# Moving the modulation vector of a transformer kernel from its own TensorE stage into the mixing stage, on VectorE

## The chip, the cores and the metric

One NeuronCore of a Trainium2 chip runs the whole kernel. The metric is the device time of one execution in microseconds (us), the median of three runs. The engines are TensorE (PE, its weight loads PEld), VectorE (DVE), ScalarE (ACT), GpSimd (POOL) and the sync engine (SP), which issues the weight transfers in program order.

## The reference, cut to what matters

256 tokens of width 1024 pass through two blocks. All is float32.

```
h = x
xn = rmsnorm(h); proj = xn @ w_in                  # "mixing": attention and a gated recurrence
h = h + concat(attn, rec) @ w_out                  # outproj
hn = rmsnorm(h)
# PEER: product keys, top 16 of 8 heads -> 128 rows of u and of v for every token
eidx, gates = topk(hn @ wq, subkeys)
act = gelu(sum_d(hn * u[eidx]));  h = h + sum_k(gates * act * v[eidx])
h = rmsnorm(h)
# second block, two layers, each modulated by six vectors that depend on c alone
m = silu(c) @ ada_w + ada_b                        # [1024] @ [1024, 6144], once for each layer
x = modulated mixer, modulated swiglu (layer 0) ; modulated attention, modulated swiglu (layer 1)
```

The change concerns `m`. It needs only `c` and two matrices of 25 MB each, and is first used behind the PEER stage.

## The kernel before

Features lie on the 128 partitions, tokens on the free axis. Weights come in units of 1 MB (2048 columns on 128 partitions) or 1.5 MB (3072 columns) into `ring`, which has four slots. SP loads unit g when unit g-4 has been used (`wait_slot`, semaphore `unit_done`). The list `LAYERS` gives the order: `inproj` is units 0 to 13, `outproj` 14 to 17, `peerq` 18 to 25, `ada` 26 to 57, and then the second block.

**Mixing.** PE works through units u = 0 to 13: `unit_start(u)`, then `features` or `rows` (32 passes of 128x256), then for u from 4 on a `level(u-4)` of the recurrence and pieces of the attention: `at_transpose`, `at_scores`, `at_out`. On DVE a loop over u from 4 to 13 goes beside it: read the bank of unit u, `level_diff(i+1)`, `level_keep(i)` with i = u-4, `at_logits(u-8)`, `at_norm(u-9)`; behind the loop stand `at_norm(5)`, four `at_store` and the recurrence's output. ACT takes exponentials (`level_exp`, `at_exp`), POOL two products for each level (L363, L364). Ahead of the loop, DVE forms the forget gates (from L755) once ACT has read units 2 and 3, and `level(0)` hangs on these.

**Outproj, peerq.** DVE adds each outproj unit to `hT` (L887); `norm(1)` follows, then eight peerq units, transposes, and the scores (L1398).

**Top-k and gather.** DVE finds the top 16 for both halves of the tokens. POOL then fetches rows by indirect DMA (L381), 512 times 128 rows of 4 KB into `rows`, a ring of 12 buffers: phase 0 and 2 from `u_d` (DVE L960), phase 1 and 3 from `v_d` (DVE L968). A buffer is refilled when DVE has used it. The first 12 are fetched while DVE is still busy with the second half's top-k.

**Modulation before.** Behind the scores PE runs 32 `ada` units: eight matmuls of one column of `silc` against 384 columns of weights (L1411), giving one row of 384 in PSUM; ACT copies it (L534), and three matmuls with one partition turn it into three columns (L1420, into `psum[:, MCOL_AT+...]`). DVE adds the bias to the 96 columns after phase 0 (L986) and forms four gains (L989).

```
dve.wait_ge(row_in[n % GRING], 16 * (n // GRING + 1))
v.tensor_tensor_reduce(row, row, xrow[tt], 1.0, 0.0, ALU.mult, ALU.add, S["act"][:, tt, k:k + 1])
```

Of the kernel before, what the change touches and what calls it, by code (L numbers as in the profile page):

```python
# [40 lines left out]
LAYERS = [("inproj", 14), ("outproj", 4), ("peerq", 8), ("ada", 32), ("l0in", 10), ("l0out", 4),  # L41
# [6 lines left out]
UNIT_COLS = {"ada": 3072, "ffn0": 3072, "ffn1": 3072}  # L48
RING = 4
RING_COLS = 3072  # L50
ADA_COLS = 384
GRING = 12
SPLIT0 = UNIT0["l0in"]
MCOL_AT = 4 * 512
# [20 lines left out]
def build(nc, xT, cols_d, w_d, alibi_d, masks_d, ident_d, tri_d, blk_d, sbmask_d, iota_d, subk_d, rg_d,  # L75
          u_d, v_d, out):
    with ExitStack() as ctx:
# [15 lines left out]
        ring = sb("ring", [P, RING, RING_COLS])  # L93
# [13 lines left out]
        ARENA = 32000  # L107
# [4 lines left out]
        def place(base, items, on=arena):  # L112

            at, arena = base, on
            for name, shape, *dt in items:
# [6 lines left out]
                elif len(shape) == 3:  # L122
# [15 lines left out]
        place(0, [("qpT", (16, 256))])  # L138
        place(0, [("acc", (2, 1024)), ("rows", (GRING, 1024)),
                  ("idx", (2, 128), I32), ("gates", (2, 128)), ("act", (2, 128)), ("gel", (128,)),  # L140
                  ("wts", (2, 128)), ("tiny", (64,)),
                  ("mrow", (2, 384)), ("s0", (16, 128)), ("s1", (16, 128)), ("s2", (16, 128)),
# [3 lines left out]
                  ("e2", (128,)), ("subk", (16, 128)), ("iota", (16,))])  # L146
# [35 lines left out]
        def col(name, i=0, n=1):  # L182
# [32 lines left out]
        silc_ready, mrow_ready, mcol_ps, mcol_ready, lam_a, lam_b = (sem(n) for n in (  # L215
            "silc_ready", "mrow_ready", "mcol_ps", "mcol_ready", "lam_a", "lam_b"))
# [70 lines left out]
        def _(sp):  # L287
            def load(u, g, src, it=0):

                sp.dma_start(ring[:, g % RING, 0:src.shape[-1]], src).then_inc(landed[g % RING], 16)  # L290

            def wait_slot(g, it=0):
# [4 lines left out]
                if b >= SPLIT0:  # L297
# [6 lines left out]
                    return  # L304
                sp.wait_ge(unit_done, it * 4 + (b + 1))
# [3 lines left out]
            for j in range(UNITS["inproj"]):  # L309
                wait_slot(j)  # L310
                load(0, j, w_d["inproj"][j])
            for name in ("outproj", "peerq"):
# [93 lines left out]
        def _(act):  # L406
# [31 lines left out]
            def split(g, it=0):  # L438
# [4 lines left out]
                a.activation(r32(S[f"whi{g % 2}"]), ring[:, g % RING, 0:2048], ACT.Copy).then_inc(w_hi, 1)  # L443

            def split_down(f, j, it=0):
                g = UNIT0[f"ffn{f}"] + j
                if j >= 2:
                    act.wait_ge(ffn_used, it * 4 + down_done(f, j - 2))
                a.activation(r32(S[f"dhi{j % 2}"]), ring[:, g % RING, 2048:3072], ACT.Copy).then_inc(d_hi, 1)  # L449
# [77 lines left out]

            G0 = UNIT0["ada"]

            def ada_row(j, u, it):  # L530
                act.wait_ge(unit_done, it * 4 + (G0 + u + 1))
                if not isinstance(j, int) or j >= 2:
                    act.wait_ge(mcol_ps, it * 4 + (u - 1))
                a.activation(S["mrow"][0:1, u % 2, :], bank[(G0 + u) % 2][0:1, 0:ADA_COLS], ACT.Copy  # L534
                             ).then_inc(unit_out[(G0 + u) % 2], 1)
# [4 lines left out]
            for j in range(4):  # L540
                ada_row(j, j, 0)
            looped(act, 4, 32, ada_row)
# [17 lines left out]
            norm(3, H_F, UNIT0["ada"], shift=mcol[:, 0:8])  # L560
# [147 lines left out]
        def _(dve):  # L708
# [20 lines left out]
            def split(g, it=0):  # L729

                dve.wait_ge(w_hi, it * 4 + (g - SPLIT0 + 1))
                v.tensor_tensor(r32(S[f"wlo{g % 2}"]), ring[:, g % RING, 0:2048], S[f"whi{g % 2}"],  # L732
                                ALU.subtract).then_inc(w_lo, 1)

            def split_down(f, j, it=0):
                g, n = UNIT0[f"ffn{f}"] + j, FU * f + j
                dve.wait_ge(d_hi, it * 4 + (n + 1))
                v.tensor_tensor(r32(S[f"dlo{j % 2}"]), ring[:, g % RING, 2048:3072], S[f"dhi{j % 2}"],  # L738
                                ALU.subtract).then_inc(d_lo, 1)

# [12 lines left out]
            norm(0, col("norm1", 0, 8), xn)  # L753
            dve.wait_ge(lam_b, 1)
# [82 lines left out]
            for u in range(4, 14):  # L837
# [11 lines left out]
                if i < 7:  # L849
                    level_diff(i + 1)  # L850
# [820 lines left out]
```

## Time and profile before

| | us |
|---|---|
| median of 3 runs (1816.78 to 1818.4) | 1817.16 |
| the profiled execution's own time | 1817.12 |
| its span, first to last instruction | 1815.3 |
| mixing, outproj, peerq and scores | 0 to 284 |
| top-k on DVE, beside the first modulation units on PE | 281 to 386 |
| gather phases 0, 1, 2, 3 on DVE, ends | 595, 761, 927, 1092 |
| second block | 1092 to 1815 |

Over the span PE is busy 60%, DVE 65%, ACT 22%, POOL 29%. These shares mix stages with different limits, so each stage is read by itself. The 1.8 us between span and time lie around the first and last instruction.

### The profile page before, as it was taken

Reading aid. Unit: us, or ns where it says so; the run is one execution under the profiler, and the core shown is the slowest. Engines: PE = TensorE matmul, PEld = TensorE weight load, DVE = VectorE, ACT = ScalarE, POOL = GpSimd, SP = SyncE. Lnnn points to the kernel's source line nnn. Section 1 sums busy time; section 2 is a strip of 40 time slices with the busy share of each in tenths; the row PEclk is TensorE's granted clock in tenths of the full one; section 3 lists DMA queues with packets and bytes.
Section 4 is the critical chain, followed back from the end, with each engine's and each line's share of the span. In section 5 each row is a group of like instructions: output and inputs, shape, how many; then the busy total and the mean of one; then the engine's idle time right before and its main releaser. Section 6 shows DMA issues by size and latency. Waiting matters only on the chain.

```text
span 1815.3 us, 18389 instructions
## 1 busy us (share of the span) xinstructions
PE 1093.3 (60%) x6880; PEld 906.4 (50%) x6880; DVE 1178.7 (65%) x1764; ACT 404.2 (22%) x588; POOL 529.0 (29%) x566
## 2 busy tenths in 40 slices
PE   8896999999400000000000006968999897979998
PEld 7785784333100000000000005968999896779998
DVE  1353107993699999999999995564454535654544
ACT  2113101000000000000000003534444455644442
POOL 1220000232477777677777750000000000200000
PEclk9897999999755555555555557988999998999999
DMA  6221355899999999999999992443444343034550
GB/s 253 92 99 46 116 186 217 337 374 419 414 409 410 409 410 409 409 410 409 410 402 410 410 360 68 160 168 122 180 173 171 118 163 140 1 139 174 177 188 39
DMA packets 93947, 453.89 MB, mean 250 GB/s; under 512 B 10496, under 2 KB 10640, under 8 KB 76480
## 3 DMA queue, kind: packets, MB, share of 16 engines
q0 software_dynamic: 74448, 272.67, 37.7%
q1 hardware_dynamic: 19440, 180.48, 26.9%
q8 instruction: 32, 0.52, 0.1%
q14 instruction: 27, 0.22, 0.0%
HBM read 452.06 MB, written 1.05 MB: 250 GB/s over the span
## 4 chain that ended last, share of the span: by engine, by line
PE 45%; DMA 26%; DVE 17%; POOL 4%; issue 4%; ACT 4%; POOLq 0%; DVEq 0%; SPq 0%; ACTq 0%
DMA arena<-u_d,arena 15%; PE psum L1477 14%; DMA arena<-v_d,arena 11%; PE psum L1217 7%; PE psum L1243 7%; PE psum L1491 7%; DVE psum L968 4%; POOL arena L381 4%; PE psum L1226 2%; DVE arena L960 2%; PE psum L1201 2%; PE psum L1256 1%; ACT whi L443 1%; DVE arena L907 1%; DVE arena L898 1%
## 5 line engine op out<-in xcount | busy, mean ns | idle before, releaser
L1437 PE MATMUL psum<-ident,arena 128*128 128x128 f32 x16 | 3.9, 426 | 616.7 <-DVE arena L960 451.2
L960 DVE CUSTOM_DVE_ANT_0 arena<-arena,psum 128x1024 f32<-128x1024 f32 x256 | 310.5, 1220 | 60.5 <-DMA arena<-u_d,arena 50.3
L381 POOL DMA_INDIRECT arena<-u_d,arena x256 | 239.8, 937 | 292.5 <-DVE arena L960 123.0
L968 DVE SCALAR_TENSOR_TENSOR psum<-arena,psum 128x1024 f32<-128x1024 f32 x252 | 321.0, 1288 | 2.2 <-DMA arena<-v_d,arena 2.2
L1437 PEld LDWEIGHTS psum<-ident,arena 128*128 128x128 f32 x16 | 3.1, 224 | 617.1 <-issue 451.2
L732 DVE TENSOR_TENSOR wlo<-ring,whi 128x2048 fp32r<-128x2048 f32 x74 | 169.9, 2298 | 163.3 <-ACT whi L443 163.3
L381 POOL DMA_INDIRECT arena<-v_d,arena x256 | 239.7, 936 | 91.9 <-issue 44.8
L1477 PE MATMUL psum<-xh,whi 128*128 128x256 f32 x704 | 201.1, 286 | 9.8 <-DVE xl L726 9.8
L1477 PE MATMUL psum<-xl,whi 128*128 128x256 f32 x704 | 200.9, 285 | 0.0
L1477 PE MATMUL psum<-xh,wlo 128*128 128x256 f32 x704 | 200.7, 285 | 0.0
L1411 PE MATMUL psum<-ring,silc 128*1 128x384 f32 x512 | 170.1, 486 | 0.0
L443 ACT ACTIVATE whi<-ring 128x2048 fp32r<-128x2048 f32 x74 | 140.5, 1900 | 39.6 <-PE psum L1243 39.6
L1477 PEld LDWEIGHTS psum<-xh,whi 128*128 128x128 f32 x704 | 136.8, 194 | 10.5 <-issue 10.5
L1477 PEld LDWEIGHTS psum<-xl,whi 128*128 128x128 f32 x704 | 136.9, 194 | 0.0
L1477 PEld LDWEIGHTS psum<-xh,wlo 128*128 128x128 f32 x704 | 136.8, 194 | 0.0
L738 DVE TENSOR_TENSOR dlo<-ring,dhi 128x1024 fp32r<-128x1024 f32 x44 | 53.9, 1224 | 103.5 <-ACT dhi L449 103.5
L1217 PE MATMUL psum<-xn,ring 128*128 128x256 f32 x512 | 113.9, 385 | 3.2 <-DVE xn L716 3.2
L1217 PEld LDWEIGHTS psum<-xn,ring 128*128 128x128 f32 x512 | 98.8, 194 | 17.6 <-issue 4.0
L555 ACT ACTIVATE arena<-arena 128x128 f32<-128x128 f32 x2 | 0.6, 310 | 449.5 <-DVE arena L960 449.5
L1491 PE MATMUL psum<-fh,dhi 128*128 128x256 f32 x352 | 99.7, 283 | 0.0
L1491 PE MATMUL psum<-fl,dhi 128*128 128x256 f32 x352 | 99.6, 283 | 0.0
L1491 PE MATMUL psum<-fh,dlo 128*128 128x256 f32 x352 | 99.6, 283 | 0.0
(231 smaller groups left out, 2112.4 us busy)
## 6 DMA issues: line engine op xcount, KB each, us to landing
ring<-w_ffn SPq DMA_DIRECT2D x44, 1536.0 KB, 6.3
ring<-w_ada SPq DMA_DIRECT2D x32, 1536.0 KB, 9.1
ring<-w_inproj SPq DMA_DIRECT2D x14, 1024.0 KB, 4.8
ring<-w_qkv SPq DMA_DIRECT2D x12, 1024.0 KB, 4.7
ring<-w_l0in SPq DMA_DIRECT2D x10, 1024.0 KB, 6.3
ring<-w_peerq SPq DMA_DIRECT2D x8, 1024.0 KB, 4.8
ring<-w_outproj SPq DMA_DIRECT2D x4, 1024.0 KB, 4.7
arena<-u_d,arena POOLq DMA_INDIRECT x256, 12.6
```

The costliest lines, as they stand in the source:

```text
L381: g.indirect_dma_start(S["rows"][:, n % GRING, :], None, table, bass.IndirectOffsetOnAxis(S["idx"][:, tt, k:k + 1], 0)).then_inc(row_in[n ...
L443: a.activation(r32(S[f"whi{g % 2}"]), ring[:, g % RING, 0:2048], ACT.Copy).then_inc(w_hi, 1)
L732: v.tensor_tensor(r32(S[f"wlo{g % 2}"]), ring[:, g % RING, 0:2048], S[f"whi{g % 2}"], ALU.subtract).then_inc(w_lo, 1)
L738: v.tensor_tensor(r32(S[f"dlo{j % 2}"]), ring[:, g % RING, 2048:3072], S[f"dhi{j % 2}"], ALU.subtract).then_inc(d_lo, 1)
L960: v.tensor_tensor_reduce(row, row, xrow[tt], 1.0, 0.0, ALU.mult, ALU.add, S["act"][:, tt, k:k + 1]).then_inc(rows_used, 1)
L968: v.scalar_tensor_tensor(vacc[k % 2], row, w, vacc[k % 2], ALU.mult, ALU.add).then_inc(rows_used, 1)
L1201: ins = t.matmul(NORM[:, 0:T], ones[:, :], sq[:, k, :], start=(k == 0), stop=(k == KT - 1))
L1217: ins = t.matmul(bank[g % 2][:, b * T:(b + 1) * T], w[:, b, k, :], src[:, k, :], start=(k == 0), stop=(k == KT - 1))
L1243: ins = t.matmul(bank[g % 2][:, b * T:(b + 1) * T], r32(w[i][:, b, k, :]), r32((hi, lo)[j][:, k, :]), start=(k == 0 and i + j == 0), stop= ...
L1411: ins = t.matmul(bank[g % 2][0:1, 0:ADA_COLS], silc[:, k:k + 1], w[:, k, :], start=(k == 0), stop=(k == KT - 1))
L1477: ins = t.matmul(bank[g % 2][:, b * T:(b + 1) * T], r32(w[i][:, b, k, :]), r32((xh, xl)[jj][:, k, :]), start=(k == 0 and i + jj == 0), sto ...
L1491: ins = t.matmul(bank[2 + n // 2][:, 256 * (n % 2):256 * (n % 2) + 256], r32(w[i][:, n, :]), r32(S[f"{('fh', 'fl')[jj]}{u % 2}"]), start=( ...
```

## The change

The `ada` units leave `LAYERS`, so that `l0in` follows `peerq`. Their matrices come as 64 half units of 0.75 MB (four groups of 384 columns) into five slots of their own, `ada_slot`, each counted by `ada_in`. DVE multiplies and accumulates: for unit m, eight instructions over 384 columns, the first a `tensor_scalar`, the others `scalar_tensor_tensor` that wait for the one before (`ada_mac`), into one of two accumulators. PE then sums over the partitions with three matmuls of the accumulator against one column of ones (`ada_columns`, counted by `mcol_ps`); an accumulator is free again when that is done. `ADA_AT` says how many halves DVE does in each unit g: 6 ahead of the forget gates (g=3), 3 for each g from 4 to 12, 6 for 13, 2 for 14 to 18, 3 for 19 to 23. SP loads them between the weight units.

```diff
-LAYERS = [("inproj", 14), ("outproj", 4), ("peerq", 8), ("ada", 32), ("l0in", 10), ...
+LAYERS = [("inproj", 14), ("outproj", 4), ("peerq", 8), ("l0in", 10), ...
+ADA_HALF = 4 * ADA_COLS
+ADA_RING = 5
+ADA_AT = {3: 6, **{g: 3 for g in range(4, 13)}, 13: 6, **{g: 2 for g in range(14, 19)}, **{g: 3 for g in range(19, 24)}}
+ADA_DONE = {g: sum(n for at, n in ADA_AT.items() if at <= g) for g in range(-1, 27)}
+ADA_EARLY = {4: 6, 5: 8, 6: 10, 7: 11, 17: 39}
@@ SP
+            def load_ada(upto):
+                while ada_next[0] < min(upto, 2 * ADA_UNITS):
+                    i = ada_next[0]
+                    if i >= ADA_RING:
+                        sp.wait_ge(ada_mac, 4 * (i - ADA_RING + 1))
+                    sp.dma_start(ada_slot[i % ADA_RING], ...).then_inc(ada_in[i % ADA_RING], 16)
+                    ada_next[0] += 1
+                    wait_slot(g)
+                    load(0, g, w_d[name][j])
+                    if g == 3:
+                        load_ada(ADA_RING)
+                    if g >= 4:
+                        load_ada(ADA_EARLY[g] if g in ADA_EARLY else ADA_DONE[g - 5] + ADA_RING)
@@ ACT: ada_row and its loop are gone
@@ DVE
+            def ada_halves(n):
+                for i in range(ada_next[0], ada_next[0] + n):
+                    m, w, acc = i // 2, ada_slot[i % ADA_RING], ada_acc[i // 2 % 2]
+                    dve.wait_ge(ada_in[i % ADA_RING], 16 * (i // ADA_RING + 1))
+                    if i % 2 == 0 and m >= 2:
+                        dve.wait_ge(mcol_ps, m - 1)
+                    for j in range(4):
+                        k = 4 * (i % 2) + j
+                        wk = w[:, ADA_COLS * j:ADA_COLS * (j + 1)]
+                        if k == 0:
+                            v.tensor_scalar(acc, wk, silc[:, k:k + 1], None, ALU.mult).then_inc(ada_mac, 1)
+                        else:
+                            dve.wait_ge(ada_mac, 8 * m + k)
+                            v.scalar_tensor_tensor(acc, wk, silc[:, k:k + 1], acc, ALU.mult, ALU.add
+                                                   ).then_inc(ada_mac, 1)
             norm(0, col("norm1", 0, 8), xn)
+            ada_halves(ADA_AT[3])
             dve.wait_ge(lam_b, 1)
...
                 if i < 7:
                     level_diff(i + 1)
+                ada_halves(1)
                 if i < 8:
                     level_keep(i)
...
+                ada_halves(1)
                 if 0 <= u - 8 < 6:
                     at_logits(u - 8)
                 if 0 <= u - 9 < 6:
                     at_norm(u - 9)
+                ada_halves(1)
+            ada_halves(2)
             at_norm(5)
             for i in (2, 3, 4, 5):
                 at_store(i)
+                if i == 3:
+                    ada_halves(1)
...
             for j in range(4):
                 g = UNIT0["outproj"] + j
+                ada_halves(ADA_AT[g])
                 dve.wait_ge(unit_done, g + 1)
...
             norm(1, col("norm2", 0, 8), xn)
+            for g in range(UNIT0["peerq"], UNIT0["peerq"] + 6):
+                ada_halves(ADA_AT[g])
+            (bias and gains, moved here from behind phase 0)
@@ PE
+            def ada_columns(g, units=None):
+                for m in range(ada_next[0], ADA_DONE[g] // 2 if units is None else units):
+                    pe.wait_ge(ada_mac, 8 * m + 8)
+                    for c in range(3):
+                        at = MCOL_AT + 3 * m + c
+                        ins = t.matmul(psum[:, at:at + 1], ada_acc[m % 2][:, c * P:(c + 1) * P], ones[:, 0:1],
+                                       start=True, stop=True)
+                    ins.then_inc(mcol_ps, 1)
+                    ada_next[0] = m + 1
                     rows(u, xn)
+                ada_columns(u - 1)
                 if u >= 4 and u - 4 < 9:
                     level(u - 4)
...
+            ada_columns(13, 17)
             at_transpose(4)
             at_out(3)
             at_transpose(5)
             at_out(4)
+            ada_columns(13, 18)
...
                 features(g, S["cat"])      # outproj; for peerq likewise
+                ada_columns(g - 1)
...
-            ada_unit, ada_column and their loop
```

In the arena, `rows` moves behind the other PEER tensors and three of the five slots lie at its top; the other two lie behind `ring`'s first-block slots, which are now 2048 columns apart. The first `l0in` units are loaded when peerq and the modulation are done.

## Rows read from the trace of the kernel before

**Rows 1.** Busy time by stretch: PE, PEld, DVE, ACT, POOL, granted PE clock, DMA share, GB/s.
```profile
0.00:283.80 283.80, 247.76 (x1215) 215.25 (x1216) 67.12 (x139) 58.89 (x115) 28.78 (x31) 0.93 0.37 134
283.80:386.00 102.20, 102.20 (x375) 33.70 (x374) 100.96 (x402) 8.83 (x19) 11.36 (x12) 1.00 0.80 309
386.00:484.00 98.00, 90.18 (x335) 30.49 (x333) 49.92 (x84) 9.26 (x20) 37.47 (x40) 0.97 1.00 409
484.00:594.70 110.70, 0.00 (x0) 0.00 (x0) 106.14 (x175) 0.00 (x0) 80.54 (x86) 0.50 1.03 409
594.70:1092.20 497.50, 1.94 (x8) 1.57 (x8) 487.07 (x529) 1.90 (x3) 350.19 (x374) 0.50 1.01 402
```

**Rows 2.** Timeline of DVE, start and duration, at both ends of phase 0.
```profile
385.98 1.21 DVE L960 CUSTOM_DVE_ANT_0 arena<-arena,psum 128x1024 f32<-128x1024 f32 x1
387.12 1.22 DVE L960 CUSTOM_DVE_ANT_0 arena<-arena,psum 128x1024 f32<-128x1024 f32 x1
...
594.63 0.28 DVE L974 TENSOR_REDUCE arena<-arena 128x8 f32<-128x128 f32 x1
...
595.83 0.26 DVE L986 TENSOR_TENSOR mcol<-psum,cols 128x96 f32<-128x96 f32 x1
```

**Rows 3.** DMA queue of SP's transfers between 386 and 484: packets, MB, share.
```profile
q1 hardware_dynamic: 2299, 23.00, 56.6%
```

**Rows 4.** Timeline of POOL: the first row fetched once DVE uses buffers.
```profile
388.61 0.94 POOL L381 DMA_INDIRECT arena<-u_d,arena  x1 [39.55 <-DVE arena L960]
```

**Rows 5.** Timeline of DVE at 384 columns, layer 1.
```profile
1527.09 0.55 DVE L1163 SCALAR_TENSOR_TENSOR second<-psum,second 128x384 f32<-128x384 f32 x1
1527.67 0.56 DVE L1168 TENSOR_TENSOR second<-second 128x384 f32<-128x384 f32 x1
1528.15 0.55 DVE L1169 SCALAR_TENSOR_TENSOR second<-psum,second 128x384 f32<-128x384 f32 x1
```

**Rows 6.** Groups of DVE instructions by shape: count, busy us, mean ns.
```profile
L716 DVE SCALAR_TENSOR_TENSOR sq<-hT,gain,rstd 128x256 f32<-128x256 f32 x32 | 13.0, 478 | 16.4 <-ACT rstd L428 16.4
L1152 DVE SCALAR_TENSOR_TENSOR second<-second,cols 128x512 f32<-128x512 f32 x4 | 2.8, 748 | 5.7 <-ACT second L669 5.7
L1064 DVE TENSOR_SCALAR second<-second,cols 128x256 f32<-128x256 f32 x4 | 1.1, 345 | 0.0
```

**Rows 7.** Timeline of PE: level(0), the peerq units, a modulation unit's columns.
```profile
52.93 2.08 PE L1276 MATMUL psum<-arena 128*128 128x128 f32 x8 [4.25 <-POOL arena L364]
...
219.59 55.49 PE L1217 MATMUL psum<-xn,ring 128*128 128x256 f32 x256 [1.62 <-DVE xn L716]
...
294.49 0.82 PE L1420 MATMUL psum<-ones,arena 1*128 1x1 f32 x6
295.24 5.32 PE L1411 MATMUL psum<-ring,silc 128*1 128x384 f32 x16
```

**Rows 8.** Timeline of DVE: the first instruction of the forget gates.
```profile
42.53 0.17 DVE L755 TENSOR_SCALAR small<-small 128x4 f32<-128x4 f32 x1 [26.00 <-ACT small L466]
```

**Rows 9.** Busy time by stretch, columns as in the first group: unit 8's read to the last at_store.
```profile
95.85:172.56 76.71, 67.82 (x368) 57.99 (x366) 32.61 (x66) 20.87 (x48) 8.41 (x6) 0.91 0.24 83
```

**Rows 10.** Timeline of DVE: first and last of the four outproj additions.
```profile
192.33 0.69 DVE L887 TENSOR_TENSOR hT<-psum,hT 128x512 f32<-128x512 f32 x1 [12.45 <-PE psum L1217]
...
213.05 0.69 DVE L887 TENSOR_TENSOR hT<-psum,hT 128x512 f32<-128x512 f32 x1 [6.21 <-PE psum L1217]
```

**Rows 11.** DMA issues: count, KB of each, median us from issue to landing.
```profile
ring<-w_ffn SPq DMA_DIRECT2D x44, 1536.0 KB, 6.3
...
ring<-w_peerq SPq DMA_DIRECT2D x8, 1024.0 KB, 4.8
```

**Rows 12.** Timeline of DVE and of POOL, both on SBUF operands, in layer 1.
```profile
1539.17 1.08 DVE L1168 TENSOR_TENSOR second<-second 128x384 f32<-128x384 f32 x1
...
1542.67 1.01 POOL L402 TENSOR_TENSOR second<-second 128x256 f32<-128x256 f32 x1 [2.84 <-ACT second L687]
```

**Rows 13.** Busy time by stretch, columns as in the first group: behind the mixing loop.
```profile
156.00:168.00 12.00, 9.94 (x43) 7.97 (x42) 4.33 (x16) 3.32 (x11) 0.00 (x0) 0.52 0.00 0
```

More of the change, by code:

```diff
@@ L38 @@
 NEG = -1e30
-LAYERS = [("inproj", 14), ("outproj", 4), ("peerq", 8), ("ada", 32), ("l0in", 10), ("l0out", 4),
+LAYERS = [("inproj", 14), ("outproj", 4), ("peerq", 8), ("l0in", 10), ("l0out", 4),
           ("ffn0", FU), ("qkv", 12), ("l1out", 4), ("ffn1", FU)]
@@ L90, in build, with slot @@
         NORM = bank[7]
-        ring = sb("ring", [P, RING, RING_COLS])
+        ring = sb("ring", [P, RING * RING_COLS])
+        def slot(g, lo, hi):
+            base = (g % RING) * (2048 if g < SPLIT0 else RING_COLS)
+            return ring[:, base + lo:base + hi]
         hT = sb("hT", [P, KT, T])
@@ L145, in build @@
                   ("posb", (128,), U32), ("fa", (128,)), ("fb", (128,)), ("e1", (128,)),
-                  ("e2", (128,)), ("subk", (16, 128)), ("iota", (16,))])
+                  ("e2", (128,)), ("subk", (16, 128)), ("iota", (16,)),
+                  ("rows", (GRING, 1024))])
+        ADA_TOP = ARENA - 3 * ADA_HALF
+        ada_slot = [ring[:, RING * 2048 + ADA_HALF * i:RING * 2048 + ADA_HALF * (i + 1)] for i in range(2)] + \
+                   [arena[:, ADA_TOP + ADA_HALF * i:ADA_TOP + ADA_HALF * (i + 1)] for i in range(3)]
+        ada_acc = [ring[:, 11264 + ADA_COLS * i:11264 + ADA_COLS * (i + 1)] for i in range(2)]
         S["oh"] = S["s2"].rearrange("p a b -> p (a b)").rearrange("p (a b) -> p a b", b=16)
@@ L308, in _ @@
             sp.dma_start(hT[:, :, :], xT).then_inc(x_in, 16)
[L309 to L312, printed above, removed]
+            for name in ("inproj", "outproj", "peerq"):
                 g0 = UNIT0[name]
                 for j in range(UNITS[name]):
-                    wait_slot(g0 + j)
-                    load(0, g0 + j, w_d[name][j])
-            for name in ("ada", "l0in", "l0out", "ffn0", "qkv", "l1out", "ffn1"):
+                    g = g0 + j
+                    wait_slot(g)
[4 more added lines that the diff above has]
+                        load_ada(ADA_EARLY[g] if g in ADA_EARLY else ADA_DONE[g - 5] + ADA_RING)
+            load_ada(2 * ADA_UNITS)
+            sp.wait_ge(unit_done, SPLIT0)
+            sp.wait_ge(ada_mac, 8 * ADA_UNITS)
+            sp.wait_ge(mcol_ps, ADA_UNITS)
+            for name in ("l0in", "l0out", "ffn0", "qkv", "l1out", "ffn1"):
                 g0, n = UNIT0[name], UNITS[name]
@@ L442, in split @@
                     act.wait_ge(unit_done, it * 4 + (g - 1))
-                a.activation(r32(S[f"whi{g % 2}"]), ring[:, g % RING, 0:2048], ACT.Copy).then_inc(w_hi, 1)
+                a.activation(r32(S[f"whi{g % 2}"]), slot(g, 0, 2048), ACT.Copy).then_inc(w_hi, 1)
             def split_down(f, j, it=0):
@@ L448, in split_down @@
                     act.wait_ge(ffn_used, it * 4 + down_done(f, j - 2))
-                a.activation(r32(S[f"dhi{j % 2}"]), ring[:, g % RING, 2048:3072], ACT.Copy).then_inc(d_hi, 1)
+                a.activation(r32(S[f"dhi{j % 2}"]), slot(g, 2048, 3072), ACT.Copy).then_inc(d_hi, 1)
             def read_unit(g, fn, dst, **kw):
@@ L558, in _ @@
             split(SPLIT0 + 1)
-            norm(3, H_F, UNIT0["ada"], shift=mcol[:, 0:8])
+            norm(3, H_F, UNIT0["l0in"], shift=mcol[:, 0:8])
             G0 = UNIT0["l0in"]
@@ L888, in _ @@
             norm(1, col("norm2", 0, 8), xn)
+            for g in range(UNIT0["peerq"], UNIT0["peerq"] + 6):
+                ada_halves(ADA_AT[g])
+            dve.wait_ge(mcol_ps, ADA_UNITS)
+            seq.mark(v.tensor_tensor(mcol[:, :], psum[:, MCOL_AT:MCOL_AT + 96], col("adab", 0, 96), ALU.add))
+            seq.wait()
+            for i, (n, c) in enumerate((("mix0", 8), ("ffng0", 32), ("mix1", 56), ("ffng1", 80))):
+                v.scalar_tensor_tensor(gain[:, i, :], mcol[:, c:c + 8], 1.0, col(n, 0, 8), ALU.add, ALU.mult
+                                       ).then_inc(mcol_ready, 1)
             def top16(vals, work, top, pos, n):
@@ L1221, in rows @@
             def rows(g, src):
-                w = ring[:, g % RING, 0:2048].rearrange("p (b k c) -> p b k c", b=2, k=KT)
+                w = slot(g, 0, 2048).rearrange("p (b k c) -> p b k c", b=2, k=KT)
                 for tt in range(TT):
```

83 lines of the change are left out of this document (29 added, 54 removed).

## The prediction

> **What bounds the kernel now.** I read the stages first, then the timelines of DVE and PE at each joint, then the DMA queues. Up to 284 us PE works nearly without a break and the transfers use a third of the queues' time; from 284 to 386 DVE is busy with the top-k; from 386 on the 16 DMA engines are full, at 402 to 410 GB/s [rows 1]. So a microsecond of PE or DVE in the mixing stage is paid in full, and in the gather a byte is. The modulation stage lies across this border. PE does it beside the top-k, for nothing; but between 386 and 484 its weights, and the first `l0in` units queued behind them, moved 23.0 MB against the gather [rows 3]. DVE was busy only 50 of those 98 us, against 106 of the next 111 [rows 1].
>
> **The saving.** Phase 0 ran from 385.98 to 594.63, 208.6 us for 128 rows [rows 2]. A row is 128 x 4 KB = 524,288 bytes, at 409 GB/s 1.28 us. Without the other traffic: twelve rows lie ready, and DVE takes one in 1.14 us (the step between its first two). POOL issues the thirteenth at 388.6 [rows 4]; with its 0.9 us and an estimated 2.5 us to land, the other 116 follow at 1.28, so the last is there at 388.6 + 3.4 + 148.5 = 540.5, and DVE is done at 541.8: 52.8 us less. Bounds: no use of the full ring, 128 x 1.28 = 164, saves 44.7; DVE alone as the limit, 128 x 1.14 = 146, saves 62.5. I take 52.8, nearest to how phase 2 behaves with full queues. Bias (0.26) and the four gains behind phase 0 take about 0.7 more [rows 2]; moved, they lie beside the last peerq unit. Together 53.5. The 23.0 MB say the same: 56 us at 409 GB/s [rows 3]. What of the stage ran beside the top-k gives nothing back.
>
> **Price of a half unit.** 224 of the 256 new DVE instructions are `scalar_tensor_tensor` over 384 columns that wait for the one before. At 256 columns with a pointer scalar one takes 0.478, at 512 0.748 [rows 6]: between them 0.613 at 384. From start to start, an instruction that waits for its forerunner comes 0.58 behind it, one that doesn't 0.48, for a duration of 0.55 [rows 5]: a dependent one costs duration + 0.03. So 0.645 each, 0.585 if pointer scalars cost no more than those rows. The `tensor_scalar` is 0.42 (0.345 at 256 columns [rows 6], scaled, plus the wait). A half is 3 x 0.645 + 0.42 = 2.36 or 4 x 0.645 = 2.58, mean 2.47; all 64 take 158 us.
>
> The Trainium skill, VectorE: DVE Perf Modes, section "The DRAIN you can't avoid", says that a semaphore behind each operation costs nothing extra. The trace disagrees by the 0.10 us of [rows 5]; by the page a half would be 0.4 shorter and the sum some 8 us lower (a rival below).
>
> **Price of a column group.** Three matmuls with weights of one partition take 0.75 (294.49 to 295.24) [rows 7]. With 128 partitions I take the same; below, 0.5; above, 1.1.
>
> **The mixing stage, step by step**, each by the shift it adds.
>
> 1. *Forget gates, +11.9.* DVE must do six halves before L755. Half 4 opens unit 2, whose accumulator is free only when PE has summed unit 0. PE does that after `features(4)`, which ends at 52.93 - 4.25 = 48.68 [rows 7]; with the columns 49.4, then 4.94 for halves 4 and 5: 54.4 instead of 42.53 [rows 8]. Everything up to `level(0)` and unit 5 hangs behind it, ACT and POOL too; SP is also held at half 9, whose slot is half 4's, but units 4 to 6 are already loaded.
> 2. *Units 5 to 7, +2.3.* DVE has room (its halves fall into waits for PE), PE doesn't: three column groups.
> 3. *Units 8 to 13, +12.* Before, from unit 8's read to the last `at_store` it was 76.7 us, with DVE busy 32.6 [rows 9]. The 21 halves 18 to 38 are put in: 32.6 + 21 x 2.47 = 84.5. DVE is now the limit, about 12.9 us for a unit instead of 10. `at_norm(5)` and `at_store(2)` stand behind five halves with `at_out(3)` and `at_out(4)` waiting for them, and half 38 waits for columns that PE issues after `at_out(4)`: some 4.3 us of waits in the tail. 88.8 - 76.7 = 12.
> 4. *Outproj, +9.4.* Half 39 must precede the first addition, but SP issues it with g = 18, that is after unit 14 is done. 1 MB lands in 4.8, 0.5 MB more takes 1.5 [rows 11]: half 39 is there 7 after unit 14. Then two halves and the addition (0.7), 12.6 after the unit instead of 0.1. From there additions follow at 5.6, until the fourth waits: half 46 needs the columns of unit 21 behind unit 17. First unit to fourth addition: 7 + 4.9 + 0.7, then unit 16, columns, unit 17, columns (2 x 7.66), then 2.4 + 0.7 = 31.0; before, 213.05 - 192.33 + 0.9 = 21.6 [rows 10].
> 5. *Peerq, +8.5.* Seventeen halves are 42 us and eight units 55.5 [rows 7], so PE is the limit: ten column groups, 7.5, and about 1 of waits where a half is not ready.
>
> Sum 44.1. For DVE and POOL on SBUF together I add 2: a product of 0.56 took 1.08 on DVE when POOL's began beside it, or POOL's took 1.01 [rows 12], and six of POOL's pairs will now meet halves. Shift 46. With all low prices (0.585, 0.5, no sharing) it is 37; with all high (0.70, 1.1, 340 GB/s for single transfers, sharing at each meeting) 58.
>
> Time: 1817.12 - 53.5 + 46 = 1809.6, against the profiled execution's own time, which is 0.04 from the median of the runs. The second block and phases 1 to 3 keep their lengths; ACT loses 32 copies that nothing waited for.
>
> **Rivals.**
> - *PE at its low clock* (slower). In 156 to 168, with waits of 2 to 4 us ahead and between, the granted clock was 0.52, the 1.2 GHz level, and matmuls took twice their time [rows 13]. The change puts waits of 1 to 4 us into units 10 to 13 and outproj. At the low level a unit's PE work is about 18 instead of DVE's 12.9: +5 for each of three; outproj's units 15 to 17 lose 4 each: 27 in all, 1837. It decides from 11 us on, two loop units and one outproj unit. Against it: in rows 9 the mean was 0.91 with gaps of up to 4. The Trainium skill, TensorE: Matmul & The Clock Gate, Part 1, has the clock fall back after idleness; by it this is likelier than the mean suggests.
> - *No change.* The shift is 52 or more, by contention and late halves, and the ring's start saves 49 to 53: 1816 to 1820. For it: every term of the shift is a chain of waits in which a slip adds.
> - *Cheap accumulation.* Pointer scalars and columns cost their low prices: 1801.
> - *Semaphore free.* Dependent steps as independent ones (the page's rule above): 1817.1 - 53.5 + 38 = 1801.6. Rows 5 speak against it.
> - *Hidden early wait.* If the first columns came in PE's stall earlier, step 1 would vanish: 1798. The program order of PE excludes it.
>
> **Numbers.** Forecast 0.56; low clock 0.14; no change 0.14; cheap 0.11; semaphore 0.03; others 0.02. What a measurement of this kernel can tell from no change is 0.2%, 3.6 us. The forecast's own range is 1802 to 1817; of its 0.56, 0.44 is below 1813.5, 0.10 within 0.2%, 0.02 above. Faster 0.44 + 0.11 + 0.03 + 0.01 = 0.59; within 0.2% 0.10 + 0.12 = 0.22; slower 0.19. Range for 8 in 10: from 1798 (shift 37 with the middle saving is 1800.6) to 1826 (shift 58 with the low saving is 1830, half the low-clock case is 1823).
>
> **What the profile after would show.** L755 at 54 instead of 42.5, or step 1 is wrong. Start steps of 0.645 in `ada_halves`. Units 9 to 13 12 to 13 us apart, DVE without waits. First outproj addition 12 to 13 behind its unit, waiting for a DMA. First top-k instruction at 327 (281 before). Phase 0 of 156 us, with DVE waiting for u rows only in snatches. A PE clock near 0.5 in units 10 to 17 would bear out the first rival. The prediction fails if the shift passes 54 or phase 0 stays over 165.

## The result: 1% slower, and the profile after

The changed kernel took 1836.5 us (median of 4 runs, 1827.34 to 1837.21) against 1817.78 (4 runs) of the kernel before on the same chip: ratio 1.0096, 95% interval 1.0070 to 1.0122. Its median is 18.7 us slower; 1809.6 was forecast, and 1836.5 lies above the range. The profiled execution took 1836.16, its span is 1834.0.

Timeline of DVE at the first top-k instruction, before:

```profile
281.19 3.19 DVE L894 MAX8 arena<-arena 128x8 f32<-128x128 f32 x16 [58.98 <-ACT arena L538]
```

The same after, then both ends of phase 0 (they answer to [rows 2]).

```profile
349.90 2.22 DVE L962 MAX8 arena<-arena 128x8 f32<-128x128 f32 x11 [12.40 <-ACT arena L571]
...
454.69 1.21 DVE L1028 CUSTOM_DVE_ANT_0 arena<-arena,psum 128x1024 f32<-128x1024 f32 x1
...
613.03 0.28 DVE L1042 TENSOR_REDUCE arena<-arena 128x8 f32<-128x128 f32 x1
```

Two differences carry the result. The top-k starts at 349.90 instead of 281.19: the mixing stage became 68.7 longer (46 was predicted). Phase 0 lasts 158.6 instead of 208.9, and bias and gains (0.7) are hidden: 51.0 come back (53.5 predicted). 68.7 - 51.0 = 17.7 of the 19.0 between the profiled executions' times (1836.16 and 1817.12).

Busy time by stretch, after; columns as in [rows 1]. The first ends with unit 8, the second with the last `at_store` (it answers to [rows 9]), the third at the top-k.

```profile
0.00:110.50 110.50, 83.94 (x404) 74.63 (x404) 63.51 (x107) 18.48 (x28) 21.10 (x23) 0.91 0.72 282
110.50:216.70 106.20, 86.49 (x435) 75.41 (x433) 85.46 (x158) 20.87 (x48) 10.02 (x6) 0.81 0.53 205
216.70:349.90 133.20, 112.96 (x548) 99.00 (x549) 69.03 (x123) 17.85 (x36) 1.13 (x2) 0.91 0.60 233
...
454.60:613.00 158.40, 0.00 (x0) 0.00 (x0) 153.34 (x256) 1.99 (x4) 117.53 (x126) 0.50 0.99 393
```

Against the steps of the prediction, the shift divides as follows; ends of units are start plus duration of their last matmuls.

| stretch | before | after | shift | predicted |
|---|---|---|---|---|
| to the end of unit 8 | 95.8 | 110.6 | 14.8 | 14.2 (steps 1, 2) |
| from there to the last `at_store` | 76.8 | 106.1 | 29.3 | 12 (step 3), 2 for sharing |
| from there to the end of unit 14 | 19.6 | 18.9 | -0.7 | 0 |
| unit 14 to the fourth addition | 21.6 | 32.3 | 10.7 | 9.4 (step 4) |
| fourth addition to the top-k | 67.5 | 82.0 | 14.5 | 8.5 (step 5) |

In the second stretch DVE was busy 85.46 us, 84.5 was predicted. It was not the limit all the way, however: it stood still for over 20 us, 17 of them in waits of more than 0.3, where 4.3 were allowed. These waits, total, times and longest:

```profile
DVE ring L786 <- PE psum L1397: 4.9, 2, 4.0
DVE arena L855 <- PE psum L1357: 4.0, 1, 4.0
DVE arena L897 <- PE psum L1287: 4.0, 2, 3.0
DVE arena L882 <- PE psum L1385: 2.1, 1, 2.1
DVE arena L885 <- PE psum L1385: 2.1, 1, 2.1
```

They are all for PE: 12.2 us fall behind the end of unit 13 (185.5), in the tail, and 4.9 ahead of it. PE's timeline shows why it was late:

```profile
114.78 1.44 PE L1397 MATMUL psum<-ones,ring 128*128 128x1 f32 x6 [3.62 <-DVE ring L789]
116.08 3.76 PE L1342 MATMUL psum<-arena 128*128 128x128 f32 x16
119.77 2.07 PE L1357 MATMUL psum<-arena 64*128 64x256 f32 x4
121.77 8.67 PE L1287 MATMUL psum<-ring,xn 128*128 128x256 f32 x32
130.28 0.72 PE L1397 MATMUL psum<-ones,ring 128*128 128x1 f32 x6
130.87 2.03 PE L1342 MATMUL psum<-arena 128*128 128x128 f32 x16
132.83 1.13 PE L1357 MATMUL psum<-arena 64*128 64x256 f32 x4
133.88 7.17 PE L1287 MATMUL psum<-ring,xn 128*128 128x256 f32 x32
...
204.42 1.94 PE L1385 MATMUL psum<-arena 128*64 128x128 f32 x8 [6.53 <-DVE arena L882]
```

The first row is the column group of unit 8, which waits 3.62 us for a half that DVE is still working on. Behind it the group, the level, the scores and part of the unit take about twice their time; the same four behind a group that didn't wait (130.28) take 0.72, 2.03, 1.13 and 7.17. PE is at its low clock: granted were 0.50 from 114.8 to 123.0, the 1.2 GHz level, and 1.00 from 130.3 to 141.0. So the wait of 3.62 costs another 0.7 + 1.7 + 0.9 + 1.5 = 4.8. The same happens at 145.52 (wait 3.90, granted 0.50 from 145.5 to 152.0) and through the tail. The Trainium skill, TensorE: Matmul & The Clock Gate, Part 1, has the clock fall back after idleness; the trace agrees in these places.

The tail had a low clock before the change too. Busy time from the end of unit 13 to the last `at_store`, columns as above, before and then after:

```profile
150.98:172.56 21.58, 14.57 (x77) 12.15 (x76) 5.68 (x17) 7.92 (x23) 0.00 (x0) 0.68 0.14 49
185.54:216.66 31.12, 19.51 (x93) 16.79 (x93) 18.12 (x39) 7.92 (x23) 0.00 (x0) 0.62 0.35 135
```

What is new there is that DVE has 12 us more to do and waits for the slow PE in between.

The half at the first wait was late in part because one ahead of it had been stretched; DVE's own timeline shows this together with POOL's:

```profile
104.07 4.46 DVE L789 SCALAR_TENSOR_TENSOR ring<-ring,silc 128x384 f32<-128x384 f32 x4
...
105.32 1.26 POOL L404 TENSOR_TENSOR arena<-arena 128x512 f32<-128x512 f32 x1 [7.85 <-ACT arena L514]
106.54 1.58 POOL L405 TENSOR_TENSOR arena<-arena 128x512 f32<-128x512 f32 x1
```

One line's instructions in that stretch, durations min/median/max in ns:

```profile
L789 DVE SCALAR_TENSOR_TENSOR ring<-ring,silc x4: 610/1059/1626, 104.1 to 107.0; 128x384 f32<-128x384 f32 x4
```

Four accumulation steps take 4.46 instead of 2.58. The first two take 0.6. The third starts at 105.37, just behind POOL's first product, and ends at 106.99, 0.41 after that product's end; the fourth starts at 107.0, while the second product runs, and ends at 108.53, again 0.41 after its end. So a step that starts while POOL reads SBUF stands until POOL's instruction is over, and POOL's second product, 1.58 instead of 1.26, stood through the third step. It is the same in all nine accumulation steps of the kernel that took over 0.7 us: each ends 0.41 or 0.42 us behind the end of a product of POOL's. The half lost 1.9 us by it, of the 3.62 that PE then waited. The Trainium skill, SBUF — State Buffer, section Who interferes with whom, states just this: a VectorE instruction with two SBUF inputs contends with a GpSimd one that reads SBUF, and the holder keeps the ports for its whole instruction. The trace agrees here.

Outproj went nearly as predicted. Half 39 landed 6.8 behind unit 14, and the fourth addition ended 32.3 behind it (31.0 predicted); DVE's rows answer to [rows 10]:

```profile
242.41 2.58 DVE L789 SCALAR_TENSOR_TENSOR ring<-arena,silc,ring 128x384 f32<-128x384 f32 x4 [18.43 <-DMA arena<-w_ada]
...
247.20 0.68 DVE L947 TENSOR_TENSOR hT<-psum,hT 128x512 f32<-128x512 f32 x1
...
267.25 0.68 DVE L947 TENSOR_TENSOR hT<-psum,hT 128x512 f32<-128x512 f32 x1
```

In `norm(1)` and peerq the clock again, on PE; they answer to [rows 7]:

```profile
268.44 5.27 PE L1262 MATMUL psum<-sq,ones 128*128 128x256 f32 x16 [3.60 <-ACT sq L465]
...
317.58 1.44 PE L1397 MATMUL psum<-ones,ring 128*128 128x1 f32 x6 [3.56 <-DVE ring L789]
318.88 9.09 PE L1278 MATMUL psum<-xn,ring 128*128 128x256 f32 x32
```

The norm's matmuls took 5.27 (3.72 before), and the unit behind the 3.56 of waiting 9.09 instead of 7.15. Wait and low clock are 1.6 + 3.6 + 0.7 + 1.9 = 7.8 of the 14.5, most of the rest is the ten column groups; waits of about 1 had been allowed.

### The profile page after: what moved, and what is told of

Same layout as the page of the kernel before. It is cut to its first block, busy times and chain, and to the rows that moved or that the text cites. A ratio compares the mean times of both kernels' runs of the same rounds, so it can differ in the third digit from the quotient of the medians.

```text
span 1834.0 us, 17354 instructions
## 1 busy us (share of the span) xinstructions
PE 940.2 (51%) x6368; PEld 879.3 (48%) x6368; DVE 1328.1 (72%) x2020; ACT 389.0 (21%) x556; POOL 532.5 (29%) x566
## 4 chain that ended last, share of the span: by engine, by line
PE 43%; DVE 20%; DMA 19%; POOL 8%; issue 5%; ACT 3%; SPq 0%; POOLq 0%; DVEq 0%; ACTq 0%
PE psum L1531 14%; DMA arena<-v_d,arena 11%; POOL arena L422 8%; DMA arena<-u_d,arena 7%; PE psum L1304 7%; PE psum L1545 6%; PE psum L1278 6%; DVE arena L1028 4%; PE psum L1262 2%; DVE psum L1036 2%; DVE ring L789 2%; PE psum L1287 2%; PE psum L1317 1%; ACT whi L484 1%; DVE arena L975 1%
## 5 line engine op out<-in xcount | busy, mean ns | idle before, releaser
L1278 PEld LDWEIGHTS psum<-xn,ring 128*128 128x128 f32 x512 | 98.8, 195 | 17.3 <-issue 4.0
L789 DVE SCALAR_TENSOR_TENSOR ring<-arena,silc,ring 128x384 f32<-128x384 f32 x133 | 85.0, 639 | 24.2 <-DMA arena<-w_ada 19.5
```

The lines of the kernel that those rows point to most:

```text
L789: v.scalar_tensor_tensor(acc, wk, silc[:, k:k + 1], acc, ALU.mult, ALU.add).then_inc(ada_mac, 1)
L1278: ins = t.matmul(bank[g % 2][:, b * T:(b + 1) * T], w[:, b, k, :], src[:, k, :], start=(k == 0), stop=(k == KT - 1))
```

## The experiments

All interval ratios are against the kernel before on the same chip, which ran between 1816.31 and 1817.18. Ends of unit 8, of the last `at_store`, and the first top-k instruction, from the profiled executions, with the window between the first two:

| kernel | unit 8 | `at_store` | window | top-k |
|---|---|---|---|---|
| before | 95.8 | 172.6 | 76.8 | 281.2 |
| after | 110.6 | 216.7 | 106.1 | 349.9 |
| before, products cut | 89.7 | 166.4 | 76.7 | 275.0 |
| after, products cut | 103.4 | 200.3 | 96.9 | 333.1 |
| before, fillers | 91.3 | 167.7 | 76.4 | 274.7 |
| after, fillers | 109.7 | 206.6 | 96.9 | 339.9 |
| after, both | 106.7 | 200.1 | 93.4 | 333.6 |
| before, products on VectorE | 93.4 | 170.3 | 76.9 | 279.0 |
| after, products on VectorE | 113.7 | 214.0 | 100.3 | 346.6 |
| after, halves before the gates fewer | 105.6 | 204.4 | 98.8 | 337.5 |
| after, redistributed twice | 104.9 | 193.0 | 88.1 | 311.2 |

**The changed kernel again.**

> The changed kernel once more, as the yardstick for the others of this group. Both theories: 1836, with the peerq units ending 69 us later than before and the first gather phase 50 us shorter. If one of its runs lies near 1827 again, the difference between its runs is a matter of when TensorE's clock falls.

1833.62 us (1830.13 to 1836.53), ratio 1.0088 [1.0064, 1.0111]. The changed kernel spreads over 1827 to 1837, more than most of the others. The parts of its two profiled executions agree: the window of the table is 106.1 and 106.2, the top-k comes at 349.9 and 350.2.

**The saving: the modulation's work left out** (no loads, halves or columns; the vectors are twice the bias).

```diff
-                while ada_next[0] < min(upto, 2 * ADA_UNITS):
+                while False:
-                for i in range(ada_next[0], ada_next[0] + n):
+                for i in range(0):
```

> The changed kernel without its modulation work: no loads of the matrices, no halves, no column sums; the six vectors are twice the bias instead (left out: silu(c) @ ada_w). Everything else stays. This is the saving by itself. The prediction's step: 53.5 us, 1763. From the profile after, where phase 0 took 158.4 us instead of 208.6 and the bias block is gone behind it: 51 us, 1765. If the rival of a small saving held: 45, 1771.

1767.29 us, ratio 0.9725 [0.9708, 0.9741]. Transposes at 275.36, phase 0 from 386.42 to 544.37, 158.0 us. Against the kernel before that is 49.9 less, where 53.5 was predicted; everything else is the shift.

**Low clock: fillers.** Matmuls of `ones` against `xn` into a bank that nobody reads, where PE waits.

```diff
+            def fill(n):
+                for _ in range(n):
+                    t.matmul(NORM[:, 0:T], ones[:, :], xn[:, 0, :], start=True, stop=True)
+                    fill({8: 8, 11: 9}.get(m, 0))
                     pe.wait_ge(ada_mac, 8 * m + 8)
+                fill({5: 9, 13: 7}.get(u, 0))         # ahead of level(u - 4)
             at_transpose(4)
+            fill(14)
```

> Dummy products of ones and xn into an unused part of PSUM, 8 and 9 ahead of the waits for the columns of units 8 and 11, 9 and 7 ahead of level(1) and of the last transposes in the loop, and 14 behind at_transpose(4), where PE waited 3.5 to 6.5 us; TensorE has more work, the outputs are the same. Clock theory: what the prediction missed in the mixing stage is the time at 1.2 GHz behind these waits (levels, scores and the next unit at twice their length), so the kernel gets 8 to 14 us faster, to 1822 to 1828, and the last at_store moves from 217 to about 205. Sharing theory (VectorE's accumulation is stretched by GpSimd's products on the same SBUF): PE's clock is not what sets the path, so 1836 or 1 to 3 more for the added work.

1824.78 us (1823.62 to 1826.41), ratio 1.0043 [1.0026, 1.0060]. Extra work on PE took about 9 us off. The PE timeline shows the first of the waits filled, and the level, scores and unit behind it at 2.03, 1.13 and 7.17:

```profile
110.09 3.70 PE L1392 MATMUL psum<-xn,ones 128*128 128x256 f32 x16
113.84 0.83 PE L1403 MATMUL psum<-ones,ring 128*128 128x1 f32 x6
114.53 2.03 PE L1342 MATMUL psum<-arena 128*128 128x128 f32 x16
116.50 1.13 PE L1357 MATMUL psum<-arena 64*128 64x256 f32 x4
117.55 7.17 PE L1287 MATMUL psum<-ring,xn 128*128 128x256 f32 x32
```

The control has 38 fillers in the waits that the kernel before already had, ahead of `level(0)` (7) and `level(1)` (9), of `at_transpose(4)` (8) and of the transposes for outproj (14).

> The same fillers in the kernel before, which has nearly the same four waits (4.25, 4.20, 4.22 and 6.78 us). It tells how much of a filler's gain belongs to the change. Before, level(1) took 3.12 instead of 2.1, the tail's transposes 1.09 instead of 0.6, unit 14 some 2 too long: clock theory 1812 to 1814, 3 to 5 us less; so that of the 9 us that fillers gave in the changed kernel about half is the change's own. If fillers cost as much as they give here: 1817.

1811.81 us, ratio 0.9976 [0.9966, 0.9985]: 5 us less. None of it lies in the window of the table (76.4 against 76.8), while in the changed kernel 9.2 do. So fillers help both kernels, and the gain between unit 8 and the last `at_store` belongs to waits that the change brought or made dearer.

**VectorE beside POOL: POOL's 16 level products cut to 8 columns** (the recurrence is then not the reference's; of the two lines one is shown), in the kernel after and, as control, before.

```diff
-                g.tensor_tensor(kd[:, :, 0, :], kk[:, :, 0, :], E[:, :, 0, :], ALU.mult).then_inc(hg_kq, 1)
+                g.tensor_tensor(flat(S[f"K{i % 2}"])[:, 0:8], flat(S["kk"])[:, 0:8], flat(S[f"D{i % 2}"])[:, 0:8], ...
```

> GpSimd's sixteen products of the recurrence levels are cut to 8 columns each (the recurrence is then wrong, all instructions and waits stay). In the profile after, a half unit beside such a pair took up to 4.9 us instead of 2.6; the excess sums to 8.9 us, of which 6 stood on the path. Sharing theory: 6 us for the sharing and 4.8 for the two pairs that stand on the path themselves (ahead of level(0) and level(1)), and fewer waits of PE for columns: 1836 - 11 to 15 = 1821 to 1825. Clock theory: only the 4.8 of the pairs, which the kernel before would gain too: 1831. The halves should all be 2.3 to 2.6 us.

> Control for nopool_after: the kernel before with GpSimd's sixteen products cut to 8 columns (the recurrence is then wrong). The two pairs ahead of level(0) and level(1), 2.5 us each, stand on its path. Both theories: 1811 to 1813. What nopool_after gained beyond this (15 us against the changed kernel) belongs to the change: sharing theory 8 to 11 us, so this run gains 4 to 6. If this run gains 12 or more, the sharing has no part in it.

1818.9 us, ratio 1.0010 [0.9997, 1.0023], and for the control 1810.14, 0.9961 [0.9947, 0.9976]. Cut before, the products give 7 us; cut after, 15 to 18. The accumulation steps of the whole mixing stage by their slot, in the kernel after and then in the one with cut products (groups: count, busy us, mean ns):

```profile
L789 DVE SCALAR_TENSOR_TENSOR ring<-arena,silc,ring 128x384 f32<-128x384 f32 x133 | 85.0, 639 | 24.2 <-DMA arena<-w_ada 19.5
L789 DVE SCALAR_TENSOR_TENSOR ring<-ring,silc 128x384 f32<-128x384 f32 x91 | 62.2, 684 | 3.4
```

```profile
L789 DVE SCALAR_TENSOR_TENSOR ring<-arena,silc,ring 128x384 f32<-128x384 f32 x133 | 82.1, 617 | 24.2 <-DMA arena<-w_ada 19.4
L789 DVE SCALAR_TENSOR_TENSOR ring<-ring,silc 128x384 f32<-128x384 f32 x91 | 56.2, 618 | 3.4
```

8.9 us of DVE's time are stretch. The shift of the top-k is 58.1 with the products cut against 68.7: 10.6 go with the products. That is the stretch, the waits of PE that follow from it, and whatever their coming sooner gives; the cut doesn't tell these apart. The kernel before paid a little of it already: cutting its products took DVE's busy time in the window from 32.6 to 29.5, without making the window shorter.

**Both causes away together.**

> Both suspected causes are taken away together: POOL's 16 level products are cut to 8 columns (so the recurrence isn't the reference's), and PE has the filler matmuls in its five waits. Theory A, the two causes are separate (DVE and POOL slow each other on SBUF; PE falls to its low clock behind its waits): the filler's 9 to 12 us come on top of the 15 of the cut products, so about 1808 to 1811 us, transposes near 318, and the shift against the same cut in the kernel before (1810.1) is near 51, the net near zero. Theory B, the clock falls only because stretched halves make PE wait: with the products cut the waits are 1 to 2 us and the fillers give at most 3 us more: 1816 to 1819.

1818.67 us, ratio 1.0009 [0.9999, 1.0019]: nothing more in the time, as the second theory had it. The table says what lies behind it. In the window both together give 12.7 (106.1 to 93.4), less than 9.2 + 9.2, so the causes overlap. Split at the end of unit 13 the window shows where, in us:

| kernel | units 9 to 13 | tail, to the last `at_store` |
|---|---|---|
| before | 55.2 | 21.6 |
| after | 74.9 | 31.1 |
| after, products cut | 65.7 | 31.2 |
| after, fillers | 70.1 | 26.9 |
| after, both | 66.5 | 26.8 |

In units 9 to 13 the cut alone gives 9.2, and fillers on top give nothing: a stretched half makes PE wait, and the wait lowers the clock. With the products cut, PE's wait for the columns of unit 8 is 0.83 instead of 3.62, and the level behind it is back at 2.03. In the tail, where POOL has no products, the cut gives nothing and the fillers 4.3. Ahead of unit 8 this run is 3.3 later than with the cut alone. 2.2 of that stand already at the end of the first five units (50.5 against 48.3), ahead of the first filler, so they are not the fillers' doing; the start varies that much between executions.

**Lockout or readiness: the same products, whole, on VectorE.**

```diff
-                g.tensor_tensor(kd[:, :, 0, :], kk[:, :, 0, :], E[:, :, 0, :], ALU.mult).then_inc(hg_kq, 1)   # POOL
+                if i < 7:
+                    level_products(i + 1)         # DVE, behind level_keep(i)
```

> The changed kernel with POOL's 16 level products done by VectorE, each pair behind level_keep; the whole computation stays. Lock theory (a half that meets a POOL product stands still until it ends, and this alone is what the cut products gave beyond their own latency): no accumulation step is over 0.63 us, and DVE loses 9 us of stretch but gains 16 x 0.68 = 10.9 us of products, so the time stays within 4 us of the changed kernel, 1830 to 1837. Latency theory (the cut helped because the products came sooner, not because DVE was left alone): products at 0.68 instead of 1.5 give about half of what the cut gave, 8 us: 1825 to 1829.

> The control: the same move in the kernel before, where DVE is idle most of the mixing stage. The cut gave 7 us there (1810.1). A product pair takes 1.36 instead of 2.65 us and lies on the path of level(0) and level(1) only: 2.6 us plus what the shorter waits save of the low clock, 1811 to 1814. If a wait of DVE behind ACT's exponential delays other DVE work: no gain, 1817.

> The fastest distribution so far with the products on VectorE. There the stretch is larger (steps at a mean of 695 and 651 ns instead of 617: 13.4 us) than the 10.9 us of products that replace it, and levels 0 and 1 come sooner: 1 to 5 us less than the same without the move, 1786 to 1790. If DVE is the limit in the levels' units and the products cost it more than the lock did: 1792 to 1797.

1831.99 us, ratio 1.0082 [1.0065, 1.0099]; before 1814.28, 0.9989 [0.9979, 0.9998]; on the redistributed kernel 1794.16, 0.9876 [0.9860, 0.9893]. The steps are at their bare time again, with the whole computation kept:

```profile
L774 DVE SCALAR_TENSOR_TENSOR ring<-arena,silc,ring 128x384 f32<-128x384 f32 x133 | 82.2, 618 | 24.7 <-DMA arena<-w_ada 19.9
L774 DVE SCALAR_TENSOR_TENSOR ring<-ring,silc 128x384 f32<-128x384 f32 x91 | 56.2, 618 | 3.4
```

Yet the time hardly moves, as the lockout theory had it: 10.9 us of products replace 8.9 of stretch on DVE. The other theory had 8 us for the earlier products alone. The test isn't clean, though: unit 8 ends 3.1 later (113.7 against 110.6), and units 9 to 13 take 69.3 instead of 74.9, with DVE busy 66.1 instead of 67.2. How much of that is the lock and how much the sooner product stays open. On the redistributed kernel the move loses 3.3: the hope there was wrong. Its PE waits 7.38 us for a column group at 69.82.

**Half 39 earlier:** `ADA_EARLY[17]` from 39 to 44, so that five halves are loaded ahead of unit 17's weights.

> One number of the load order: halves 39 to 43 are issued behind outproj's last weight unit instead of behind peerq's first, so that half 39 is in SBUF when the recurrence ends. In the profile after VectorE waited 18.4 us for it, to 6.9 us behind unit 14. Step 4 of the prediction as it stands: first addition 5 us earlier (half 40 still waits for columns behind unit 14), 5 to 9 us in all, 1827 to 1831. If outproj is bound by the chain of additions and columns instead, 0 to 3 us.

1832.92 us, ratio 1.0091 [1.0074, 1.0109]: no gain beyond the spread of the changed kernel. In the profile the first of outproj's additions comes at 238.22 instead of 247.20, but the norm behind them only 5.0 earlier and its matmuls at the low clock again (5.85), and the peerq units end 4.2 earlier.

**Fewer halves ahead of the forget gates:** 4 instead of 6, the two others in unit 5.

> Four halves instead of six ahead of the forget gates, the two others in unit 5, where VectorE waited 6 us for level(1). Step 1 of the prediction: the forget gates start 12 us earlier, at 43.5. VectorE and PE are not the limit before unit 8, so most of it arrives: 9 to 12 us, 1822 to 1826. Rival: VectorE's halves in all are the limit up to outproj, and what is put off comes back: 0 to 4 us.

1827.26 us, ratio 1.0060 [1.0040, 1.0080]. 6 to 9 us less in the medians, 12.4 at the top-k. Unit 8 ends 5.0 earlier, and the window behind it is 7.3 shorter as well, 5.6 of it in units 9 to 13 (69.3 for 74.9) with all products and no filler: the halves meet the waits of PE elsewhere. So what a cut or a filler gives in these units is in part a matter of how the pieces fall, and its 9.2 or 4.8 is not a fixed price.

**Redistribution.** No halves in the tail, four behind the recurrence's output, two per later outproj unit, two ahead of `norm(1)`, 20 in peerq; for units 8 to 16 SP loads the five halves behind those of unit g-4, no longer of g-5; columns only where their halves are done.

```diff
-ADA_AT = {3: 6, **{g: 3 for g in range(4, 13)}, 13: 6, **{g: 2 for g in range(14, 19)}, **{g: 3 for g in range(19, 24)}}
+ADA_POS = {4: (2, 1, 1), 5: (2, 1, 1), 6: (1, 1, 1), 7: (1, 1, 1), 8: (0, 1, 1), 9: (1, 1, 1), 10: (0, 1, 1), ...
+ADA_AT = {3: 4, **{g: sum(p) for g, p in ADA_POS.items()}, 14: 4, 15: 2, 16: 2, 17: 2, 18: 2, **{g: 4 for g in range(19, 24)}}
-                ada_columns(u - 1)
+                ada_columns(0, COLS_A[u])
```

> The same work at other places: 4 halves ahead of the gates; 4 in units 4 and 5; 2 or 3 in units 6 to 13 and then none beside the level's products in units 8, 10, 12, 13; none in the tail; 4 behind the recurrence's output, 2 for each later outproj unit, 2 ahead of norm(1), 20 in peerq; loads up to four units ahead; a unit's columns at a place in PE's order where its halves are done. Both theories together: no wait of PE for a column, so no low clock and no late addition; what is left is PE's column time, 32 x 0.65 = 21, and 5 to 12 of sharing and small waits: shift 27 to 34 against a saving of 51, 1793 to 1800, faster than both kernels. If the stage is bound by VectorE's 158 us of halves in itself, the place doesn't matter: 1815 or more.

1804.09 us, ratio 0.9931 [0.9915, 0.9948]: faster than both kernels. Its PE still waited 5.53 for the columns of unit 7, and the unit behind took 9.21. The second version moves three groups, nine matmuls, behind the next unit:

```diff
-COLS_E = {4: 3, 5: 5, 6: 6, 7: 8, 8: 9, 9: 10, 10: 11, 11: 13, 12: 14, 13: 15}     # at the end of iteration u
+COLS_E = {4: 2, 5: 5, 6: 6, 7: 7, 8: 9, 9: 10, 10: 11, 11: 12, 12: 14, 13: 15}
```

> The redistributed halves once more, with three columns groups (units 2, 7 and 12) moved from the end of a PE iteration to behind the next unit, so that PE doesn't stand still for a half that is just being worked on (5.53 us at 100.13, 1.68 at 56.88 and 1.70 at 150.81 in the run of the first redistribution, with units at 9.21 and 8.66 instead of 7.17 behind the first two). If these waits and the low clock behind them are on the path: 4 to 9 us less than 1804.1, so 1795 to 1800, transposes at 303 to 308. If DVE bounds these units and PE would only wait elsewhere: 1803 to 1805.

> The fastest distribution once more, on the same chip as the three above: 1790 to 1796, as it ran before.

1790.6 us, ratio 0.9859 [0.9842, 0.9875], and measured a second time 1790.83, 0.9866 [0.9849, 0.9882]. The move gave 13 us, more than either theory allowed. Of the 13 between the profiled executions of 1803.3 and 1790.3 us, 10.7 lie ahead of the end of unit 8 (110.64 to 99.98), where the wait of 5.53 was. Windows of the first profile of this kernel, unit 8 to the last `at_store` and on to the top-k:

```profile
104.90:193.00 88.10, 75.33 (x421) 64.49 (x420) 70.17 (x130) 20.88 (x48) 10.40 (x6) 0.92 0.64 224
193.00:311.20 118.20, 108.39 (x560) 96.32 (x561) 85.70 (x151) 17.85 (x36) 1.14 (x2) 0.96 0.73 276
```

The clock is 0.92 and 0.96 where it was 0.81 and 0.91. The first window holds less work too, DVE busy 70.2 instead of 85.5, since most of the tail's halves have moved to outproj and peerq; so its 18 us less are not the waits alone. This execution took 1796.16, the one profiled again 1790.3: 4.9 of the difference stand at the end of unit 8, 1.7 of them in the start and 2.4 in one unit at the low clock (9.50 against 7.15). With fillers on top:

> The same with filler matmuls ahead of level(0) (7), level(1) (9), behind the loop (8) and ahead of the transposes for outproj (14), where PE waits 3.4, 4.2, 1.9 to 4.2 and 6.8 us. Clock theory: another 4 to 7 us less than the version without them, near 1792, with unit 14 at 7.2 instead of 9.8 and the tail's scores at 1.1 instead of 2.1. If the low clock in these places is off the path: no difference.

1795.66 us, ratio 0.9889 [0.9872, 0.9905]. Nothing gained, 5 us lost in the medians. The profiled executions (1793.47 against 1796.16) stand the other way round; against the one of 1790.3 unit 8 ends 2.0 later and the window is 1.3 longer. Why is open.

## Why the prediction was wrong

- **The saving** was right: 51.0 for 53.5, and 49.9 by leaving the work out. That is 2.5 of the 26.9 by which 1836.5 misses 1809.6.
- **Prices** were right: steps start 0.64 to 0.66 apart (104.07, 104.71, 105.37; 0.645 predicted), a half takes 2.58, a column group 0.72. So the rivals of the free semaphore and the cheap accumulation fall. *No change* falls as well: it had 1816 to 1820.
- **Steps 1 and 2** were right: 14.8 for 14.2; the gates come at 55.37 for a forecast of 54.4, with the whole program 1.0 later.
- **Step 3, "DVE is now the limit, about 12.9 us for a unit" with "some 4.3 us of waits in the tail", is the step that failed**, 29.3 for 12 and the 2 for sharing: 106.1 us for a predicted 88.8. DVE's load came out (85.5 for 84.5), with some luck, as 4.4 of it is stretch by POOL that was priced apart. But the step took the stage for as long as the busier engine's load, and here DVE needs columns from PE and PE needs halves from DVE. DVE waited 17.1 us for PE, not 4.3: 12.2 in the tail and 4.9 in units 9 to 13. Five units of 12.9 are 64.5, which leaves 24.3 of the 88.8 for the tail; 74.9 and 31.1 came. In the units the cut of the products brings 65.7, so what was missed there hangs on DVE and POOL meeting, with the waits and the low clock behind it. Not all of it is the lockout's own price, since moving two halves brought 69.3 with the products whole. In the tail the low clock behind PE's waits is 4.3, by the fillers. The controls gain no more than 0.4 in this window. With both causes away it is 93.4, 2.0 over in the units and 2.5 in the tail; DVE still waits 11.4 for PE there instead of 4.3, but which hand-overs these are for wasn't isolated by a run.
- **Sharing on SBUF, 2 us**, was mis-sized: 8.9 us of stretch on DVE, and 10.6 in the shift go with the products. That six of POOL's pairs would meet halves was right (nine steps beside six pairs); the price of a meeting was not. The rows from layer 1 [rows 12] already held the price, a 0.56 product at 1.08 beside POOL's; the error was to take it for mild contention. As a lockout, a pair of POOL's 1.3 us products can hold DVE for up to 2.6, and the half at 132.29, 4.93 instead of 2.58, nearly reached that (2.35).
- **Step 4** was right: 10.7 for 9.4. **Step 5** was short, 14.5 for 8.5: it allowed about 1 us of waits, and one wait of 3.56 with the low clock behind it (2.6) and the norm at the low clock (1.6) came.
- **The rival of the low clock** (0.14) gave 1837, and 1836.5 came, by luck in the number. Its mechanism was at work, its price wasn't right: it had 15 us for the units of the mixing stage, where fillers give back 9 in all, and 12 for outproj's units 15 to 17, of which one lost 1.5 (8.68 for 7.15). The number was met because the lockout, peerq's waits and the smaller saving filled up the rest. Its chance should have been higher, since all the waits that it needed stood in steps 3 to 5.

## What to carry to other kernels

Where two engines hand work to each other in small pieces, add up the waits of both and not the load of the busier one, and place the consumer's instruction where its input is already done: moving nine matmuls by one unit was worth 13 us. Count a VectorE instruction with two SBUF inputs as standing still while a product of POOL's on SBUF runs. For a wait of PE of 3 to 4 us, count the low clock behind it too, here up to 4.8 us.

## What was not expected of the hardware

- The lockout runs to the end of POOL's instruction, with 0.41 or 0.42 us from there to the end of the VectorE step, in nine of nine stretched steps. With POOL's products cut, no step is over 621 ns; with them, up to 1860. One group of steps in the units, first with the products and then with them cut:

```profile
L789 DVE SCALAR_TENSOR_TENSOR ring<-ring,silc x35: 589/619/1860, 104.1 to 199.7; 128x384 f32<-128x384 f32 x35
```

```profile
L789 DVE SCALAR_TENSOR_TENSOR ring<-ring,silc x31: 598/619/620, 100.1 to 183.1; 128x384 f32<-128x384 f32 x31
```

- 47 matmuls that nobody needs made the changed kernel 9 us faster.
- The third outproj unit took 8.68 instead of 7.15 behind waits of 1.81 and 2.16 us with a column group of 0.83 between them: shorter waits than in the other places.
